# A ring of sixteen slots instead of twelve for the expert weights of a trunk layer

## The reference

```
aff = softmax(h @ w_router)
g, idx = top_k(swapaxes(aff, 1, 2), cap)          # cap: 64 latent rows, 16 context rows of each expert
xs = h[idx]
hid = silu(xs @ w_gate[e]) * (xs @ w_up[e])
y = (hid @ w_down[e]) * g
ffn = zeros.at[idx].add(y);  x = x + g2 * rms_norm(ffn, g_post_ffn)
```

## Time and profile before

| | us |
|---|---|
| runs | 2991.12, 2994.15, 3000.06 |
| median of the runs | 2994.15 |
| profiled execution, span from the first to the last instruction (the page gives no other time of it) | 2995.6 |
| of it: busy PE, DVE, ACT, POOL | 2680.6, 1331.9, 525.4, 482.1 |
| moved by DMA over the span | 783.60 MB, mean 262 GB/s |

### The profile page before, as it was taken

The page is one execution under the profiler, slowest core; times in us unless marked ns, Lnnn a source line. Parts: engine busy times, 40 slices in busy tenths (PEclk is TensorE's granted clock), DMA queues, the critical chain, the costliest instruction groups (busy, mean ns, idle before and its releaser), DMA issues. The chain is left out here.

```text
span 2995.6 us, 60885 instructions
## 1 busy us (share of the span) xinstructions
PE 2680.6 (89%) x25988; PEld 1534.8 (51%) x25988; DVE 1331.9 (44%) x2353; ACT 525.4 (18%) x1471; POOL 482.1 (16%) x647
## 2 busy tenths in 40 slices
PE   5699999999959599999769999999999999999993
PEld 1366666666637489899634444333333332333330
DVE  1667667767546465666241114422233332222323
ACT  2100000000025355555331111100000000000001
POOL 0100000000065466665140000000000000000000
PEclk8899999999979799999879999999999999999996
DMA  9576555454366312221197888799999999999997
GB/s 409 210 227 208 189 180 197 174 207 173 138 204 129 131 45 53 61 52 40 26 366 267 307 308 324 309 402 404 404 405 404 404 394 396 404 404 403 403 413 290
DMA packets 268517, 783.60 MB, mean 262 GB/s; under 512 B 99473, under 2 KB 163112, under 8 KB 199712
## 3 DMA queue, kind: packets, MB, share of 16 engines
q1 hardware_dynamic: 257104, 724.13, 64.0%
q0 software_dynamic: 10848, 56.51, 6.4%
q10 hardware_dynamic: 368, 0.10, 0.0%
HBM read 712.59 MB, written 68.08 MB: 261 GB/s over the span
## 5 line engine op out<-in xcount | busy, mean ns | idle before, releaser
L2243 PE MATMUL oe_ps<-experts_ring,tail_arena 128*32 128x512 f32 x4096 | 502.8, 605 | 42.6 <-DMA experts_ring<-in_w_up 42.6
L478 DVE SCALAR_TENSOR_TENSOR pj_macc<-pj_mring,head_cond_t,pj_macc 128x1024 f32<-128x1024 f32 x240 | 297.1, 1279 | 182.1 <-DMA pj_mring<-in_w_ada 182.1
L2243 PEld LDWEIGHTS oe_ps<-experts_ring,tail_arena 128*32 128x32 f32 x4096 | 154.5, 111 | 338.8 <-issue 337.8
L551 PE MATMUL pj_ps<-head_hT,head_ring_in 128*128 128x320 f32 x1104 | 312.3, 436 | 6.5 <-DVE head_hT L451 4.2
L2276 PE MATMUL oe_ps<-experts_ring,oe_hidt 128*32 128x512 f32 x2880 | 312.1, 592 | 0.0
L2251 PE MATMUL oe_ps<-experts_ring,tail_arena 128*32 128x512 f32 x2048 | 274.3, 600 | 0.0
L551 PEld LDWEIGHTS pj_ps<-head_hT,head_ring_in 128*128 128x128 f32 x1104 | 210.9, 191 | 96.6 <-DVE head_hT L451 6.5
L2580 DVE SCALAR_TENSOR_TENSOR oe_hid_s<-oe_hid_s,oe_gcol_s,oe_ps 128x512 f32<-128x512 f32 x16 | 12.0, 748 | 535.6 <-ACT oe_hid_s L2426 535.6
L2322 PE MATMUL oe_ps<-experts_ring,tail_arena 128*128 128x512 f32 x520 | 232.5, 604 | 15.5 <-DMA tail_arena<-scratch_o 15.5
L551 PE MATMUL pj_ps<-pj_t,pj_s 128*128 128x320 f32 x736 | 210.4, 440 | 6.8 <-DVE pj_t L457 6.8
L2276 PEld LDWEIGHTS oe_ps<-experts_ring,oe_hidt 128*32 128x32 f32 x2880 | 110.2, 110 | 198.8 <-issue 198.8
(11 more groups left out here) (423 smaller groups left out, 3893.0 us busy)
## 6 DMA issues: line engine op xcount, KB each, us to landing
experts_ring<-in_w_gate SPq DMA_DIRECT2D x128, 1024.0 KB, 24.6
experts_ring<-in_w_up SPq DMA_DIRECT2D x128, 1024.0 KB, 26.2
experts_ring<-in_w_down SPq DMA_DIRECT2D x128, 1024.0 KB, 21.7
experts_ring<-in_w_out SPq DMA_DIRECT2D x68, 1024.0 KB, 6.9
pj_mring<-in_w_ada SPq DMA_DIRECT2D x64, 1024.0 KB, 9.5
head_ring_in<-in_w_in SPq DMA_DIRECT2D x23, 2048.0 KB, 7.9
ada_ring<-in_w_ada SPq DMA_DIRECT2D x16, 2048.0 KB, 19.8
scratch_z<-pj_stage POOLq DMA_DIRECT2D x19, 640.0 KB, 8.1
```

What stands on the lines that cost most here:

```text
L478: a = nc.vector.scalar_tensor_tensor(acc, w, scalar, acc, ALU.mult, ALU.add)
L551: mm = pe.matmul(bank(name, b)[:, 0:TH], a[:, k, :], h[:, k, :], start=(k == 0), stop=(k == KH - 1))
L2243: pe.matmul(ps[32 * i:32 * i + 32, bank, :], xe[:, k, GROUPS[i % 2]], w[:, kk * DE + 512 * (i // 2):kk * DE + 512 * (i // 2) + 512], start ...
```

## The change

Four arena tiles, 0, 1, 2 and 9, join the ring as slots 12 to 15; slab n goes into slot n mod 16. Loads 12 to 15 go into them for the first time, so they wait until the last row tile has read its constants (`h2r`) and has been routed (`routed`) instead of waiting for `slot_used`; from n = 16 on the wait is `slot_used` >= n - 15. Since 24 slabs are not a whole number of turns of sixteen slots, but 48 are, the loops of SP and PE do two experts a turn, with the first or the last expert outside. `EARLY` becomes 8 by its formula. The arena tiles that `x1` and the gains went to are ring slots now; they go to slots that the down slabs of expert 14 had, and each load waits for PE's use of that slab. `block_final` exchanges the tiles it works in.

```diff
+MORE = (0, 1, 2, 9)
+NSLOT = len(SLOTS) + len(MORE)
-FINAL_X, FINAL_G = (0, 1, 2, 5, 7), (9, 3)
+FINAL_X, FINAL_G, FINAL_F = (0, 1, 2, 3, 4), (5, 6), (7, 8, 9, 10, 11)
+FINAL_FG, FINAL_JUNK = (0, 1, 2, 9, 5), 7
...
+def slot_of(ring, arena, n):
+    i = n % NSLOT
+    return ring[:, SLOTS[i], :] if i < len(SLOTS) else arena[:, MORE[i - len(SLOTS)], :]
...
-    SLOTS_IN = len(slot_in)
+    SLOTS_IN = NSLOT
...
-            for n in range(SLOTS_IN):
-                if n >= 6:
+            for n in range(GU):
+                if n >= len(SLOTS):
+                    if n == len(SLOTS):
+                        sp.wait_ge(h2r, NT)
+                        sp.wait_ge(routed, NT)
+                elif n >= 6:
                     sp.wait_ge(w_used, NT * SLABS - 11 + n)
                 elif n >= 3:
                     sp.wait_ge(w_used, LAST * SLABS + 1)
-                load_expert(sp, weights, w_all, slot_in, 0, n, n)
-            for n in range(SLOTS_IN, GU):
-                load_expert(sp, weights, w_all, slot_in, 0, n, n, used=(slot_used, n - SLOTS_IN + 1))
-            with sp.Fori(1, NE) as e:
+                load(0, n, n)
+
+            def expert_loads(e, n, it):
                 for i in range(GU):
-                    load_expert(sp, weights, w_all, slot_in, e, i, GU + i, used=(slot_used, (e - 1) * PER + GU + i - SLOTS_IN + 1))
+                    load(e, i, n + i, used=(slot_used, n + i - SLOTS_IN + 1 + it * PER))
+                n += GU
                 for i in range(DN):
-                    load_expert(sp, weights, w_all, slot_in, e - 1, GU + i, 2 * GU + i, used=(slot_used, (e - 1) * PER + 2 * GU + i - SLOTS_IN + 1))
+                    load(e - 1, GU + i, n + i, used=(slot_used, n + i - SLOTS_IN + 1 + it * PER))
+
+            with sp.Fori(1, NE - 1, 2) as e:
+                expert_loads(e, GU, e - 1)
+                expert_loads(e + 1, GU + PER, e - 1)
+            expert_loads(NE - 1, GU + (NE - 2) * PER, 0)
...
             for t in range(NT):
-                sp.dma_start(arena[:, FINAL_X[t], :], x1_d[t]).then_inc(x1_in[t], 16)
+                sp.wait_ge(slot_used, base - DN + FINAL_X[t] + 1)
+                sp.dma_start(w_all[:, SLOTS[FINAL_X[t]], :], x1_d[t]).then_inc(x1_in[t], 16)
             for cnd in range(2):
-                sp.dma_start(arena[:, FINAL_G[cnd], :], bcast_rows(cst_d, (3 * cnd + 2) * D, D)).then_inc(g2_in, 16)
+                sp.wait_ge(slot_used, base - DN + FINAL_G[cnd] + 1)
+                sp.dma_start(w_all[:, SLOTS[FINAL_G[cnd]], :], bcast_rows(cst_d, (3 * cnd + 2) * D, D)).then_inc(g2_in, 16)
...
-            expert(1)
-            with pe.Fori(2, NE - 1) as e:
-                expert(e)
+            expert(1, GU, None)
+            with pe.Fori(2, NE - 2, 2) as e:
+                expert(e, GU + PER, e - 2)
+                expert(e + 1, GU + 2 * PER, e - 2)
+            expert(NE - 2, GU + (NE - 3) * PER, None)
```

More of the change, by code:

```diff
@@ L1991, in _, with load_expert @@
                 finish_pair(q)
-def load_expert(sp, weights, ring, slot_in, e, r, n, used=None):
+def slot_of(ring, arena, n):
+    i = n % NSLOT
+    return ring[:, SLOTS[i], :] if i < len(SLOTS) else arena[:, MORE[i - len(SLOTS)], :]
+def load_expert(sp, weights, ring, arena, slot_in, e, r, n, used=None):
     w_gate, w_up, w_down = weights
-    slot = n % len(slot_in)
-    place = SLOTS[slot]
+    slot, place = n % NSLOT, slot_of(ring, arena, n)
     e = bass.ds(e, 1)
@@ L2003, in load_expert @@
         src = w[0, e, (r // 2) * 256:(r // 2 + 1) * 256, :].rearrange("o (p k) f -> p (o k) f", p=P)
-        dst = ring[:, place, :].rearrange("p (k f) -> p k f", k=2)
+        dst = place.rearrange("p (k f) -> p k f", k=2)
     else:
         src = w_down[0, e, (r - 16) * P:(r - 15) * P, :].rearrange("o p f -> p (o f)")
-        dst = ring[:, place, :]
+        dst = place
     if used:
@@ L2116, in _, with load @@
                 sp.dma_start(crow[(2 + cnd) * KD:(3 + cnd) * KD, :], mod_d[cnd, 3 * D:4 * D].rearrange("(k p) -> k p", p=P)).then_inc(once, 16)
+            def load(e, r, n, used=None):
+                load_expert(sp, weights, w_all, arena, slot_in, e, r, n, used)
             for n in range(RING, NT * SLABS):
@@ L2285, in down @@
                     slot_ready(n0 + k, it)
[L2286 removed]
+                    w = slot_of(w_all, arena, n0 + k)
                     for c in range(3):
@@ L2371, in _, with expert @@
                 mm.then_inc(slot_used, 2)
-            def expert(e):
-                gate_up(e, GU, e - 1)
-                down(e - 1, 2 * GU, e - 1)
-            expert(1)
-            with pe.Fori(2, NE - 1) as e:
-                expert(e)
+            def expert(e, n0, it):
+                gate_up(e, n0, it)
+                down(e - 1, n0 + GU, it)
+            expert(1, GU, None)
[3 more added lines that the diff above has]
+            expert(NE - 2, GU + (NE - 3) * PER, None)
             base = GU + (NE - 2) * PER
@@ L2630, in sem @@
             return nc.alloc_semaphore("fi_" + name)
-        f, junk, fg = ring[:, 0:NT], ring[:, NT], ring[:, NT + 1:2 * NT + 1]
-        x, g2 = [arena[:, i, :] for i in FINAL_X], [arena[:, i, :] for i in FINAL_G]
+        f, x, g2 = ([ring[:, SLOTS[i], :] for i in at] for at in (FINAL_F, FINAL_X, FINAL_G))
+        fg, junk = [arena[:, i, :] for i in FINAL_FG], arena[:, FINAL_JUNK, :]
         st, eps = sb("st", [P, NT, 3]), sb("eps", [P, 1])
@@ L2641, in _ @@
             for t in range(NT):
-                sp.dma_start(f[:, t, :], ffn_d[(t - 1) % NT]).then_inc(loads[t], 16)
+                sp.dma_start(f[t], ffn_d[(t - 1) % NT]).then_inc(loads[t], 16)
             for t in range(NT):
@@ L2674, in _ @@
                 dve.wait_ge(gain_done, t + 1)
-                nc.vector.scalar_tensor_tensor(x[t], fg[:, t, :], st[:, t, 2:3], x[t], ALU.mult, ALU.add).then_inc(done, 1)
+                nc.vector.scalar_tensor_tensor(x[t], fg[t], st[:, t, 2:3], x[t], ALU.mult, ALU.add).then_inc(done, 1)
 def trunk(nc, a, s):
@@ L2724, in trunk_experts @@
         ring = ctx.enter_context(nc.sbuf_tensor("experts_ring", [P, 12, D], F32))
-        slot_in = [nc.alloc_semaphore(f"experts_slot{i}") for i in range(12)]
+        slot_in = [nc.alloc_semaphore(f"experts_slot{i}") for i in range(NSLOT)]
         res_in, ring_in = nc.alloc_semaphore("w_out_res_in"), [nc.alloc_semaphore(f"w_out_ring_in{i}") for i in range(6)]
```

10 lines of the change are left out of this document (5 added, 5 removed).

## The result

| | before | after |
|---|---|---|
| median of the runs, us | 2997.11 (2991.12 to 3000.65) | 3009.16 (3007.84 to 3011.21) |
| after over before, 95% interval | | 1.0045 (1.0032 to 1.0058) |
| profiled execution, us (its span) | (2995.6) | 3009.79 (3008.1) |
| instruction blocks moved between 1,950 and 2,900 us | 11 | 74 |

The median before is that of four runs here, one more than the prediction had (2994.15). In us the interval is 9.6 to 17.4 slower. The forecast was 2990.2, 4.0 us faster, with a range up to 2996.5: the kernel went the other way.

The account below looks back on a forecast made before the run. The DMA engines' stream of weight bytes was taken as the bound; 10.4 us gained in the hole, less 6.88 for the later release, plus 0.4 at restart, gave 4.0 us: 2990.2 us against 2994.15, range 2984.0 to 2996.5.

Parts of the forecast that it names:

- (a): Start of expert stage: loads 12 to 15 fill the DMA hole, about 1893 to 1904 us; gain 10.4 us.
- (b): Expert 0: four more sample steps precede the prompt steps, so the first slot release comes later; loss 6.88 us.
- (c): Stream restart: load 16 reaches full rate 1.55 us after issue, at 1918.2 against 1922.1; net gain 4.0 us.
- (d): Gather(1) after the prompt rows' transposes: stays in the hole; if wholly in the stream, costs 3.4 us.
- (e): PE after the restart: prompt steps end at 1928.6 us and expert 1 begins there without a wait.
- (f): Steady stage: more loads in flight gain nothing; two-expert loops cost nothing, 0 to 0.5 us either way.
- (g): The end: x1 and gains stay queued behind the last weights; PE's tail and last block keep 62.8 us.
- a full queue moves less: Rival, steady stage: SP's always full queue lowers the engines' rate by 2.1%, 21.8 us, giving 3012; chance 6%.
- A deeper queue moves bytes faster: Rival, steady stage: more loads in flight raise 421 GB/s to 427, 14 us more gained, 2976; chance 3%.
- The gains are eaten at the start: Rival, start: gather(1) falls into the stream, leaving 0.6 us of gain, 2993.5; chance 8%.
- the whole hole is won: Rival, start: the release does not come later, so the gain is 10.4 us, 2983.8; chance 7%.

Follow-up runs that it names:

- arena_once_e6: Kernel before with loads 12 to 15 put once into the four arena tiles, then twelve slots, one-expert loops, EARLY 6; 0.9977, 6.9 us under before.
- arena_once_e8: Kernel before with loads 12 to 15 put once into the four arena tiles, then twelve slots, one-expert loops, EARLY 8; 0.9988, 3.6 us under before.
- pe_half: Kernel before with PE's experts 1 to 7 written out and the one-expert loop kept for 8 to 14; 1.0017 of before, 5.1 us over.
- pe_all: Kernel before with PE's expert loop written out in full, no jump back; 1.0036 of before, 10.8 us over.
- pe_two: Kernel before with only PE's loop changed to two experts a turn; 1.0051 of before, 15.3 us over.
- after_early6: Changed kernel with EARLY 6 in place of 8, sixteen slots kept; 1.0027 of before.

## Why the prediction failed, point by point

- **(a), (b), (c), right.** Loads 12 to 15 lie in the hole, the prompt steps are where they were forecast, 3.8 us were won in the trace and 3.6 in the run that has this alone (forecast 4.0).
- **(d), right.** gather(1) ran in the hole, between 1914.3 and about 1919.
- **(e), wrong without effect.** PE came to expert 1 at 1933.2 (1928.6 and the 4.6), but waited 2.69 us there: the step left out that PE waits for `hid_done`, for ACT's and DVE's work on expert 0's result. Before, that work ended at 1932.01 and was hidden behind the wait for a load. The stream set the pace all the same: arena_once_e6 and arena_once_e8 have the same wait of 2.7 us and are below before.
- **(f), the step that failed.** "The two-expert loops halve the jumps of PE and SP and lengthen their code; ... I cost it at nothing, 0 to 0.5 us either way." I weighed the code against PE's and SP's time, which is spare, and not against the sixteen DMA engines, which are not. It cost 13 us: PE's loop was read again on every turn, 74 blocks for 11, and each block held up one of eight DMA engines by about 1.5 us. The other half of (f), that more loads in flight move no byte sooner, was right, and SP stood in the issue for about 2 us, as forecast.
- **(g), right in PE's tail (61.5 us), wrong on "behind".** x1 and the gains stayed behind the last weights in the order of issue, but 3.15 MB of them landed ahead of the last weight.

The 13 us can also be added up from the table: SP's loads fall short by 2.98 MB at 403 GB/s, 7.4 us, and 2.56 MB more of x1 and gains went ahead of the last weight at 420 GB/s, 6.1 us; together 13.5. The same sum gives 4.7 us for pe_half (measured 5.1), 11.2 for pe_all (10.8) and 13.4 for pe_two (15.3). For the change as a whole, 13.5 less the start's 4.0 is 9.5, just under the measured 9.6 to 17.4; where the rest of the median's 12 us is from stays open, and so is pe_two's 15.3.

Of the rivals, "a full queue moves less" had the sign and nearly the time (3012), and the wrong cause: with twelve loads ahead the queue isn't full and the loss is the same. "A deeper queue moves bytes faster" falls with 401 GB/s. "The gains are eaten at the start" falls with the 3.8 us, and "the whole hole is won" with the prompt steps at their forecast place; arena_once_e6, with EARLY 6, comes nearer to it (6.9 us).

The trace of before held the hint. Its 11 blocks between 1,950 and 2,900 us come until 2,052 (expert 1's own code and the loop's first turn) and from 2,858 on, with 800 us of silence between; and its spread grows from 2.2 to 3.8 us by about 2,080 and then stands nearly still until the blocks come again. Both say that one expert's code stays with PE, and that reading it in isn't free. Part 3 of the page over the stage, not over the span, is where that is seen.

The Trainium skill bears on this, "Runtime: NRT & Kernel Launch", section "Instruction fetch mechanics": it gives PE 128 KiB of instruction memory, filled in blocks of 16 KiB that the sequencer fetches over a DMA queue of its own. The runs agree with that size, which is eight blocks: a loop body of five blocks stays, one of about seven stays, one of ten is read again on every turn. The section also says that a taken branch to a target outside the current window, which it puts at two blocks, stalls until the fetch is done. The body of ten agrees, with 3.8 us at each jump; the body of five doesn't, since before jumps back with no block fetched from 2,052 to 2,858 us and no wait "<- issue". And it says that the cost of crossing into a new block is mostly hidden. For PE that holds (pe_all has no stall), but for a saturated stream of weights these runs show otherwise: about 0.2 us for each block.

## What to carry to other kernels

Where the DMA engines are the bound, reading code in takes their time too: before a loop body is doubled for a ring that doesn't divide, count its blocks and ask whether it stays with its engine; five blocks stayed, about seven stayed, ten did not, and writing the loop out in full cost most of the same (10.8 us for 15.3). A few spare tiles are worth most where there is a hole to fill, and they can be filled once without changing the ring behind them (0.9977). A share of 1.01 doesn't mean that all engines are equally far: compare the first and the last of a load's sixteen parts.

## What the runs showed of the hardware

- A block of 16 KB of code keeps its DMA engine for 1.07 us by the queue's records, but it sets one part back by 1.5 to 1.7 us, and the spread grows in steps of about 1.5 us (after_early6, the medians of eight runs of 24 loads one after the other: 3.1, 4.6, 4.6, 6.2, 7.7, 7.8, 9.4, 11.0). Which engines carry the blocks isn't in the trace. In after eight parts lag and eight don't (at the end the eighth and the ninth part lie 10.8 us apart, in the median), and the steps that were followed singly fall on late parts alone. So the blocks seem to go to one half of the engines; that it is the same half from beginning to end is argued, not shown.
- Nothing made a late engine catch up: in pe_half the spread stood at 8.3 to 8.4 us (but for the time beside each scatter) over some 330 us of full load without new code, with gathers and scatters in it. In pe_two it fell once, from 15.0 to 12.3 us between 2,757 and 2,785, but there the first parts came further apart (2.75 us for 2.48), while the last parts kept their pace of 2.48: the early engines slowed down. Why is open.
- The instruction queue's records are small beside the loss, 0.5% of the engines' time against 0.1%. The stage lost 1.3% (13.0 of 1010.7 us).
